# A fused two-block transformer kernel: 14 instead of 24 convolution taps on VectorE ahead of the attention, 16 of ScalarE's products among the query copies, the LayerNorm in ticks 33 to 42

## What is computed

```python
a = u_val * jax.nn.sigmoid(u_gate)
y = lax.conv_general_dilated(a, conv_w[:, None, :], window_strides=(1,),
    padding=[(CONV_WIDTH - 1, 0)], feature_group_count=D_CONV) + conv_b   # CONV_WIDTH = 31
y = jax.nn.silu(layernorm(y, ln_g, ln_b))
y_conv = (y @ w_pw2) * jax.nn.silu(g_conv)
...
score = jnp.einsum("bth,bths->bts", w_b, jax.nn.relu(s_raw))       # 8 index heads
_, sel = lax.top_k(score, k_top)                                   # 128 keys of each query
logits = jnp.einsum("bthc,btkc->bthk", q_b, kv_sel) * (KV_LORA ** -0.5) + bias
probs = jax.nn.softmax(jnp.where(valid, logits, -jnp.inf), axis=-1)
o = jnp.einsum("bthk,btkc->bthc", probs, kv_sel)                   # 8 heads
...
y = jnp.concatenate([y_conv, y_attn], axis=-1) @ w_out[l]
x = x + gate * rmsnorm(y, g_post[l])
```

## Time and profile before

| what | value |
|---|---|
| median of 3 runs | 1871.83 us (1871.01 to 1873.21) |
| profiled execution, its own time | 1871.72 us |
| its span | 1870.4 us |
| TensorE (PE) busy | 1663.1 us, 89% |
| VectorE (DVE) busy | 728.5 us, 39% |
| ScalarE (ACT) busy | 471.7 us, 25% |
| GpSimd (POOL) busy | 312.8 us, 17% |
| chain of waits, by engine | PE 58%, DVE 19%, DMA 18%, ACT 2% |

### The profile page before, as it was taken

How to read it: one execution, slowest core, us unless ns; L and a number is a source line. 1 busy time by engine, 2 the same in 40 slices (tenths; PEclk the granted TensorE clock), 3 DMA queues, 4 the chain that set the end, 5 groups by cost and what they waited for, 6 DMA issues and landing times.

```text
span 1870.4 us, 15310 instructions
## 1 busy us (share of the span) xinstructions
PE 1663.1 (89%) x5832; PEld 821.4 (44%) x5832; DVE 728.5 (39%) x1521; ACT 471.7 (25%) x971; POOL 312.8 (17%) x312
## 2 busy tenths in 40 slices
PE   6999957799999969898878888899989999998898
PEld 3344435664445433333333333444445544444553
DVE  2335257632234232111101110439955242996622
ACT  2001014300112110010000000546446233644721
POOL 0000000000000002111111110127415011750600
PEclk9999967899999979898888988898999999899999
DMA  8243101431454169999999999600201230030101
GB/s 312 92 178 124 57 0 63 185 135 45 146 184 179 69 262 415 399 407 404 402 401 416 403 411 385 256 0 13 101 23 46 85 107 0 1 113 23 46 1 45
DMA packets 70960, 324.30 MB, mean 173 GB/s; under 512 B 9290, under 2 KB 12626, under 8 KB 58464
## 3 DMA queue, kind: packets, MB, share of 16 engines
q1 hardware_dynamic: 63552, 308.03, 42.4%
q0 software_dynamic: 6016, 10.51, 1.8%
q10 hardware_dynamic: 1312, 4.72, 0.6%
HBM read 318.95 MB, written 12.67 MB: 177 GB/s over the span
## 4 chain that ended last, share of the span: by engine, by line
PE 58%; DVE 19%; DMA 18%; ACT 2%; issue 2%; POOL 1%; SPq 0%; DVEq 0%; ACTq 0%; POOLq 0%
PE bank L185 54%; DMA arena<-in_w 15%; DVE arena L2360 3%; DVE arena L2358 3%; DMA arena<-h_rows,arena 3%; DVE arena L2330 2%; DVE arena L2346 2%; PE bank L1945 1%; PE bank L544 1%; DVE arena L1139 1%; DVE arena L2400 0%; DVE arena L1251 0%; PE bank L628 0%; DMA arena<-in_params 0%; PE bank L828 0%
## 5 line engine op out<-in xcount | busy, mean ns | idle before, releaser
L185 PE MATMUL bank<-arena 128*128 128x512 f32 (+11 forms) x4964 | 1556.5, 556 | 98.1 <-DMA arena<-in_w 51.4
L185 PEld LDWEIGHTS bank<-arena 128*128 128x128 f32 (+2 forms) x4964 | 716.1, 183 | 868.7 <-issue 787.1
L2561 POOL TENSOR_TENSOR arena<-arena 128x512 f32<-128x512 f32 x180 | 201.2, 1118 | 233.5 <-ACT arena L2171 216.0
L1655 POOL TENSOR_TENSOR arena<-arena 128x1 f32<-128x1 f32 (+2 forms) x44 | 32.2, 733 | 730.8 <-DVE arena L1130 523.7
L1605 DVE TENSOR_TENSOR arena<-arena,bank 64x512 f32<-64x512 f32 x32 | 22.1, 691 | 314.9 <-ACT arena L1096 314.9
L2171 ACT ACTIVATE arena<-arena 128x512 f32<-128x512 f32 x180 | 126.0, 717 | 20.5 <-POOL arena L2561 20.4
L1096 ACT ACTIVATE arena<-bank 64x512 f32<-64x512 f32 x32 | 18.9, 591 | 379.9 <-PE bank L185 379.9
L909 ACT COPY arena<-bank 128x512 f32<-128x512 f32 (+2 forms) x110 | 58.8, 538 | 204.3 <-PE bank L185 171.4
L1676 POOL DMA_INDIRECT y_rows<-arena x32 | 32.1, 1004 | 413.9 <-PE bank L828 275.3
L1599 DVE COPY arena<-bank 128x512 f32<-128x512 f32 x32 | 22.2, 692 | 114.7 <-PE bank L828 108.6
L1139 DVE SCALAR_TENSOR_TENSOR arena<-arena 128x512 f32<-128x512 f32 x84 | 63.2, 752 | 3.0
(11 more groups left out here) (261 smaller groups left out, 874.8 us busy)
## 6 DMA issues: line engine op xcount, KB each, us to landing
arena<-in_w SPq DMA_DIRECT2D x96, 2048.0 KB, 36.0
arena<-in_w_in SPq DMA_DIRECT2D x15, 2048.0 KB, 8.0
arena<-in_w_ada SPq DMA_DIRECT2D x12, 2048.0 KB, 8.5
arena<-in_w_out SPq DMA_DIRECT2D x6, 2048.0 KB, 7.9
arena<-in_w_xk SPq DMA_DIRECT2D x2, 2048.0 KB, 10.8
arena<-in_w_xv SPq DMA_DIRECT2D x2, 2048.0 KB, 14.6
arena<-in_w_xq SPq DMA_DIRECT2D x2, 2048.0 KB, 8.6
arena<-in_w_xo SPq DMA_DIRECT2D x2, 2048.0 KB, 8.4
```

The source lines that it names most:

```text
L185: i = pe.e.matmul(o, l, r, start=first and j == 0, stop=last and j == len(pairs) - 1)
L2561: pool.e.tensor_tensor(yc, yc, k.prod[l][n % 4], ALU.add).then_inc(*k.pool.step("sum", l, f, j))
```

## The change

Four numbers and one loop are changed.

- `TAPS` = 14: VectorE does 14 of its taps ahead of the attention (24 before) and the 17 others one per tick in ticks 13 to 29 (7 before, in ticks 13 to 19).
- `PRODS` = 78: ScalarE does the pooled taps 62 to 77 between the query copies, two behind each of the eight, and taps 78 to 92 one per tick in ticks 14 to 28 (62 to 92 in ticks 8 to 38 before).
- `LN_AT`: the LayerNorm's five pieces lie in ticks 33, 34, 38, 41 and 42 (42, 43, 46, 48 and 49 before).

```diff
-PROD_AT, TAP_AT = 8, 13
+PROD_AT, TAP_AT = 14, 13
+PRODS, TAPS = 78, 14
...
-LN_AT = {"mu": 42, "sub": 43, "var": 46, "rstd": 48, "scale": 49}
+LN_AT = {"mu": 33, "sub": 34, "var": 38, "rstd": 41, "scale": 42}
...
-        if PROD_AT <= tick < PROD_AT + 31:
-            act_tap(k, act, l, 62 + tick - PROD_AT)
+        if PROD_AT <= tick < PROD_AT + 93 - PRODS:
+            act_tap(k, act, l, PRODS + tick - PROD_AT)
...
         act.e.activation(k.QQ[l][:, h, :], B.at("qq", l, h), ACT.Copy, scale=128 ** -0.5).then_inc(*A.step("qq", l, h))
+        act_tap(k, act, l, 62 + 2 * h)
+        act_tap(k, act, l, 63 + 2 * h)
...
-    dve_taps(k, dve, l, 0, 24)
-    dve_attend(k, dve, l, 24)
+    dve_taps(k, dve, l, 0, TAPS)
+    dve_attend(k, dve, l, TAPS)
```

## The result

| what | before | changed |
|---|---|---|
| median | 1872.12 us (4 runs) | 1892.53 us (1891.58 to 1893.67, 4 runs) |
| ratio, 95% interval | | 1.0109 [1.0092, 1.0127] |
| profiled execution | 1871.72 us | 1892.19 us |
| its span | 1870.4 us | 1890.9 us |
| TensorE busy | 1663.1 us | 1663.8 us |

A forecast was written before the change was run, and what follows sets the result against it. TensorE, busy 89% of the span, was taken to wait on VectorE before the first softmax block, in ticks 13 to 19 and at the LayerNorm. 1871.7 + 3.0 - 0.6 + 11.8 + 3.7 = 1889.6 us, range 1872 to 1898.

The forecast's parts named there:

- Part 1: Ahead of the attention: VectorE's 13 taps pair with GpSimd sums at 1.51 us, front stall grows, +3.0 us in all.
- whole instruction: Rival ahead of the attention: whole instructions exclude each other, a pair takes 1.84 us, total 1897.6 us; chance 0.05.
- Part 2: Ticks 8 to 13: ScalarE's products and the sums leave, -0.3 us per layer, -0.6 in all.
- the tap of tick 20: Tick 20: this added tap is ahead of what the transpose of tick 22 waits for, taken as 1.1 us.
- Part 3: Ticks 20 to 29: ten more taps slow VectorE's pace through tick 30, +5.9 us per layer, +11.8 in all.
- Part 4: LayerNorm moved early: its products leave waits for ticks where TensorE is full, +2.9 and +0.8 us per layer, +3.7.
- The variance, 3.5 us: LayerNorm variance: some 3.5 us of the 8.9 us moved from late waits to ticks where TensorE is full.
- The broadcast: Broadcast of the LayerNorm root: 2.0 us of the 8.9 us moved to ticks where TensorE is full.
- the clock: Rival: waits ahead of tick 44 and in ticks 20 to 30 lower the clock, 1897.6 us; chance 0.10.
- sums give way: Rival: sums yield to taps, which keep 0.79 us and fill gaps, so 1867.4 us, faster; chance 0.11.
- Only the front stall goes: Rival: the stall ahead of the first softmax block disappears, the rest as forecast, 1872.8 us, no change; chance 0.12.
- The middle is cheaper: Rival: ticks 20 to 30 cost 3.2 us per layer and the LayerNorm move 0, total 1880.5 us; chance 0.18.

The follow-up runs named there:

- experiment 1: Kernel before with only VectorE's taps split, 14 ahead of the attention and 17 in ticks 13 to 29: 1876.66 us, ratio 1.0014.
- experiment 2: Kernel before with only ScalarE's products moved as in the change, 24 taps ahead and the old LayerNorm ticks: 1895.43 us, ratio 1.0109.
- experiment 5: Changed kernel with GpSimd's 15 sums beside the taps ahead of the attention adding only 4 of 512 columns: 1883.17 us, ratio 1.0047.
- experiment 3: Changed kernel with the LayerNorm put back in ticks 42 to 49: 1887.5 us, ratio 1.0064.
- experiment 6: Changed kernel with VectorE's LayerNorm scaling in tick 43, not 42: 1893.25 us, ratio 1.0091.
- experiment 4: Kernel before with VectorE's taps in gaps: 17 ahead of the attention, 6, 3 and 5 in ticks 5, 9 and 23: 1858.72 us, ratio 0.9922.
- experiment 8: Experiment 4 with the change's placement of products, 14 taps ahead and 6, 6 and 5 in the gaps, old LayerNorm ticks: 1867.31 us, ratio 0.9962.
- experiment 7: Experiment 4 with the first gating projection in tick 2, not 1, and 15 taps ahead, 8 in tick 5: 1849.96 us, ratio 0.9881.
- experiment 9: Experiment 8 with the change's LayerNorm in ticks 33, 34, 38, 41 and 42: 1873.2 us.
- experiment 10: Experiment 9 with the output product of tick 38 moved to tick 36, away from the variance's narrow products: 1875.9 us.
- experiment 11: Experiment 10 with the root's broadcast and the scaling back in ticks 48 and 49, mean, subtractions and variance staying early: 1867.9 us.

## Why the prediction was right, step by step

**Part 1, the front: right.** What was to show it, 13 taps in 18 to 20 us, came as 19.46; 1.50 us per pair for the forecast 1.51. Experiments 1, 2 and 5 hold the cause fast: no sums, 0.78 us; 15 sums beside 23 taps, 0.72 us more for each pair; narrow sums with every product of ScalarE in place, 0.79 us. The forecast was +1.5 per layer, measured +2.6 and +2.2: the opening tap (0.54 us before, 1.45 now) and a threshold ahead of it (0.29, now 0.58) pair with the first sums too, and were left out. That depends on when the first sum begins: in experiments 3 and 6, which are the same kernel up to there, it begins behind the start of layer 1's opening tap, that tap takes 0.54 us, and the first transpose is at +1.5 and +1.4. TensorE's wait was to be 5 to 7 us; it is 8.19 in layer 1, outside that, and 6.69 in layer 2. The Trainium skill ("SBUF — State Buffer", section "SBUF: two separate sides") has the exclusion right; its "whole instruction" would be 1.84 us a pair, and the runs say 1.50.

**Part 2, ticks 8 to 13, and the tap of tick 20.** Forecast -0.3 + 1.1 = +0.8 per layer; from the first transpose to that of tick 22 it was -0.5 and +2.2, mostly clock at the second transpose (-0.8, +1.2).

**Part 3, ticks 24 to 32: right mechanism, size too large.** Forecast 4.8 per layer, measured +3.15 in both. The term that failed is "VectorE's pace goes from 2.5 to the 4.1 us": it became 3.67. Four of the six taps there start while no sum runs and take 0.74 us, the price of a tap in the lower bound of that part. The bound itself, 3.2 per layer, was for the whole part, with the tap of tick 20 (and the 4.4 - 1.4 that it names are 3.0); from the transpose of tick 20 to that of tick 32 it was +4.7 and +4.8, for the forecast 5.9. The kernel with taps in gaps shows what it is without any: nothing there, and 4 us less in ticks 13 to 19.

**Part 4, the LayerNorm: too small.** Forecast +2.9 and +0.8, measured +4.8 and +3.6 from the transpose of tick 32 to the layer's end. The mean came at 3.35 (forecast 3.4), the wait before tick 44's transpose at 4.02 (forecast "some 4 us"). Three sizes were off. "The variance, 3.5 us" was 5.3 from the transpose of tick 36 to that of tick 40: the narrow products are followed by four microseconds at 1.2 GHz, in before among waits, now where TensorE is full. The broadcast, "2.0 of the 3.4 us", cost 0.9 (from the transpose of tick 40 to that of tick 42), since in before its products ran at 1.2 GHz, which the prediction took for their price. And the end, forecast 5.8 us from the transpose of tick 44 to the first output product, is 7.6 in layer 1 and 8.0 in layer 2, since transposes and products behind the 4.02 us wait run at half the clock. (Before it is 1469.01 - 1456.18 = 12.8 in layer 1; the 1468.6 of the prediction stands in no row.) That is the rival "the clock", in the two of its places that cost something. Its low clock came in ticks 20 to 30 too, at 1431.5 us of layer 1 and at 1755.7 of layer 2, 3.4 us each, but it cost nothing there: from the transpose of tick 28 to that of tick 30 both layers, one with it and one without, are 1.14 us longer than before, and from that of tick 20 to that of tick 22 both 1.5.

For both layers, part 3 was 3.3 us too dear, part 4 4.7 and part 1 1.8 too cheap; so 17.9 became 21.2, and the errors partly cancel. The closeness of the time is in part luck: what the variance and the end cost above the forecast comes to 7.6 us in both layers, most or all of it clock, which is nearly the 8 us of the rival at 1897.6, and against it the middle and the broadcast were 5.5 us too dear. **What the rivals had right:** "sums give way" is excluded by experiments 2 and 5. "Only the front stall goes" is what the taps alone would have done, without the products; and even then 1.97 us of the stall remained, which I had not seen: VectorE's next instruction waits for scores that stand behind the gating projection. "The middle is cheaper" had the direction of part 3 right (3.2 per layer for the measured 4.7) and part 4 wrong (0 for 8.4 in both layers).

**Not settled.** Why low clock makes the ends of some layers 1 to 5 us longer than in before (experiments 1, 3 and 4, layer 1 of experiment 8) and those of others not, with the same instructions there. Every end with the late variance has some: 3.4 us in before and in experiment 7, up to 13.7 in others. Experiment 9 shows two lengths of the same piece in one execution, so it is not the order of work alone; nothing tried here controls it. No run makes the variance's products wider in the same place, so that it is their narrowness that lowers the clock is argued from where the low clock stands, not shown apart from the rest. And experiment 5 was expected to give 16 us and gave 9.4: the windows account for some 7 us lost through the clock, but the fall in tick 22 was not produced on purpose.

## What to carry to other kernels

Moving elementwise work between engines "for free" needs a look at who else uses SBUF in that stretch: a two-operand VectorE instruction of 128x512 beside such a GpSimd addition costs 0.7 us more for each pair, so put them in stretches of their own. Spread a background load by where its engine really idles (three gaps took 14 taps at no cost there; the kernel gains 0.8%, and 1.2% with the projection moved), not one per tick. When a stall at an in-order engine is shortened, look at the next instruction in its queue and at what that waits for, before counting the whole stall as gain.

## What the runs showed of the hardware

- The variance's 16 narrow products (128x1) keep TensorE busy in the trace, and low clock follows them all the same: the granted clock behind them is 0.59 and 0.55 over four microseconds, and the same dip follows them wherever they stand (0.61 and 0.53 in before, 0.58 and 0.57 in experiment 10). In both layers of all 14 kernels at least 2.5 of the four microseconds behind them are at 1.2 GHz. Ticks 32 to 40 have low clock in every layer with the variance in tick 38, 2.2 to 6.8 us of it, and none in any layer with the variance in tick 46. What lies under it takes nearly twice its time.
- A wait of 4.02 us in a stretch of short products is followed by transposes at 1.09 us for 0.60; a wait of 1.53 us in the same place (experiment 11) is followed by 0.66. Experiments 10 and 11 differ by little else, and by 8.0 us.
- A VectorE instruction with one SBUF input operand and a scalar (the opening tap) pairs with a sum as well, where a sum already runs when it starts: 1.45 us for 0.54. Where the first sum begins behind its start (experiments 2, 3 and 6, layer 1) it keeps its 0.54.
